# A layer of a hybrid decoder on one core: attention over the prompt's heads, their group norm and the output projection placed earlier in a schedule of 128 steps

## What is computed

```python
q_sb, k_sb, v_sb, q_fx, k_fx, v_fx, f = split(rms_norm(x) @ w_in)
# prompt, each head: 256 x 256 scores, stick breaking or softmax with a forget bias
o_sb = stick_breaking(q_sb, k_sb, v_sb); o_fx = forgetting(q_fx, k_fx, v_fx, cumsum(logf))
# samples: the same over cache + own token, 8 samples x 2048 past tokens x 16 heads
y = concat(rms_norm(o_sb) * g_sb, rms_norm(o_fx) * g_fx) @ w_out      # group norm, output pass
h = x + y
out = rms_norm(h + hierarchical_moe(rms_norm(h)))    # 32 experts, two for each token
# also returned: k and v of every head, prompt and sample, and the log forget values
```

## Time and profile before

| | us |
|---|---|
| median of 3 runs (1520.18 to 1528.28) | 1526.38 |
| the profiled execution, device time | 1525.93 |
| its span in the trace | 1524.2 |
| PE busy | 1339.2 (88%) |
| DVE busy | 676.4 (44%) |
| ACT busy | 243.5 (16%) |
| DMA, mean over the span | 370 GB/s |

### The profile page before, as it was taken

One profiled execution on the slowest core, in us unless ns is written; L12 is line 12 of the kernel. 1 busy time (PEld: TensorE's weight loads), 2 busy tenths in 40 slices (PEclk: granted clock), 3 DMA queues, 4 the chain that ended last, 5 costly groups with the idle time before them and its releaser, 6 DMA issues. The chain is left out here.

```text
span 1524.2 us, 27421 instructions
## 1 busy us (share of the span) xinstructions
PE 1339.2 (88%) x8718; PEld 891.7 (59%) x8718; DVE 676.4 (44%) x4802; ACT 243.5 (16%) x466; POOL 73.2 (5%) x119
## 2 busy tenths in 40 slices
PE   7999887889889889856999986889999999999992
PEld 5776554666556556523677753466567555665561
DVE  4657554676766757767655465312100100001004
ACT  2121111321321212112000011201101110111011
POOL 1000000000000000001000000101110010001000
PEclk8999999999999999977999997769999999999996
DMA  9789999999999999999899879589999999999984
GB/s 321 266 325 405 405 383 391 387 372 393 383 385 392 374 389 395 383 404 385 340 338 350 331 287 344 232 324 377 422 427 428 428 428 418 424 418 415 418 346 177
DMA packets 159080, 564.19 MB, mean 370 GB/s; under 512 B 17353, under 2 KB 59130, under 8 KB 145642
## 3 DMA queue, kind: packets, MB, share of 16 engines
q1 hardware_dynamic: 134304, 535.41, 89.6%
q10 hardware_dynamic: 21762, 22.58, 4.3%
q0 software_dynamic: 2896, 4.86, 1.0%
HBM read 551.97 MB, written 15.67 MB: 372 GB/s over the span
## 5 line engine op out<-in xcount | busy, mean ns | idle before, releaser
L132 DVE CUSTOM_DVE_ANT_0 ws<-ws,xgT 128x128 f32<-128x128 f32 x2048 | 443.3, 284 | 182.5 <-DMA ws<-in_cache_sb_k 108.1
L955 PE MATMUL bank<-xn,ws 128*128 128x264 f32 x1024 | 255.9, 406 | 4.3 <-DMA ws<-in_w_in 4.3
L955 PEld LDWEIGHTS bank<-xn,ws 128*128 128x128 f32 x1024 | 197.6, 198 | 90.9 <-issue 53.2
L1959 PE MATMUL bank<-ws,xgT 128*64 128x256 f32 x1024 | 231.1, 385 | 17.8 <-DMA ws<-in_w_expert_up 13.1
L1961 PE MATMUL bank<-ws,xgT 128*64 128x256 f32 x1024 | 231.2, 386 | 0.0
L911 PE MATMUL bank<-ws,PR 128*32 128x512 f32 x1024 | 152.4, 676 | 67.8 <-DMA ws<-in_cache_sb_v 43.6
L1959 PEld LDWEIGHTS bank<-ws,xgT 128*64 128x64 f32 x1024 | 140.0, 139 | 105.5 <-issue 21.7
L132 DVE DVE_READ_ACCUMULATOR2_ANT Z<- 128x1 f32 x2048 | 161.9, 79 | 0.0
L1961 PEld LDWEIGHTS bank<-ws,xgT 128*64 128x64 f32 x1024 | 140.3, 139 | 0.0
L2160 DVE COPY gu<-bank 128x256 f32<-128x256 f32 x32 | 13.6, 425 | 270.1 <-PE bank L1961 270.1
L1073 PE MATMUL bank<-qo,ws 128*128 128x256 f32 x512 | 118.6, 392 | 3.6 <-DVE qo L1565 3.6
(11 more groups left out here) (417 smaller groups left out, 1044.5 us busy)
## 6 DMA issues: line engine op xcount, KB each, us to landing
ws<-in_cache_sb_k SPq DMA_DIRECT2D x128, 512.0 KB, 8.6
ws<-in_cache_sb_v SPq DMA_DIRECT2D x128, 512.0 KB, 9.0
ws<-in_cache_fox_k SPq DMA_DIRECT2D x128, 512.0 KB, 8.8
ws<-in_cache_fox_v SPq DMA_DIRECT2D x128, 512.0 KB, 8.7
ws<-in_w_expert_down SPq DMA_DIRECT2D x32, 2048.0 KB, 17.0
ws<-in_w_expert_gate SPq DMA_DIRECT2D x32, 2048.0 KB, 16.0
ws<-in_w_expert_up SPq DMA_DIRECT2D x32, 2048.0 KB, 20.6
ws<-in_w_in SPq DMA_DIRECT2D x24, 2048.0 KB, 17.6
```

The costliest lines, as they stand in the source:

```text
L132: ins = dve.tensor_tensor_reduce(k, k, qb[:, m % 2, h * HD:(h + 1) * HD], 1.0, 0.0, ALU.mult, ALU.add, Z[:, m % 2, h, 2 * j + i:2 * j + i ...
L955: mm = pe.matmul(out[:, 0:T], w[:, c, m * P:(m + 1) * P], xn[:, c, :], start=(c == 0), stop=(c == KC - 1))
L1959: pe.matmul(bank[2 * k][0:SLOTS, 0:256], lhs, ws[:, wg, c * 256:(c + 1) * 256], start=(c == 0), stop=(c == KC - 1))
```

## The change

Three constants and the order of a head's pieces change.

- `UNIT0` goes from 24 to 20, so every prompt head starts four steps sooner; the last one ends in step 83 and not 87. `GSUM` goes from 89 to 85 and `OUT` from 92 to 88 with it.
- The output pass takes two of every three steps, 88, 89, 91, 92 and so on. `OUT_END`, `ROUTE` and `PLACE` stay at 111, 115 and 122.
- `ASKED` goes from 6 to 7: a query broadcast is in steps 7, 11, 15, ...
- A head's key is turned in piece 1 and its value in piece 2 (before: 0 and 1). DVE copies and ACT stores each a piece later as well, so the value's store stands in piece 3. The copies of the samples' own columns (`QK`, `VN`) move along.

```diff
-ASKED = 6
+ASKED = 7
...
-UNIT0 = 8 * (Q_TURNS + 1)
+UNIT0 = 8 * Q_TURNS + 4
...
-OUT_END = OUT + KC + KC // 4 - 1
+OUT_END = OUT + 3 * KC // 2 - 1
...
-    return d // 5 * 4 + d % 5 if 0 <= d < OUT_END - OUT and d % 5 < 4 else None
+    return d // 3 * 2 + d % 3 if 0 <= d < OUT_END - OUT and d % 3 < 2 else None
...
@@ PE, prompt_head
                     scores_read(pe, u - 1)
-                    wait_past(pe, S["row"], 2 * u)
                     z = bank[ZB]
...
+                elif piece == 1:
+                    wait_past(pe, S["row"], 2 * u)
                     rows(key)
-                elif piece == 1:
+                elif piece == 2:
                     pe.wait_ge(S["evac"], 4 * Q_TURNS + 4 * (u // 2) + u % 2 + 3)
                     pe.wait_ge(S["row"], 2 * u + 1)
                     rows(val)
-                elif piece == 2:
                     rest_read(pe, u - 1)
...
@@ ACT, prompt_head
-                elif piece == 1:
+                elif piece == 2:
                     act.wait_ge(S["row"], 2 * u + 1)
                     store(krow, fxk_p if g else sbk_p, fxk_s if g else sbk_s, h, "stk")
-                elif piece == 2:
...
+                elif piece == 3:
                     act.wait_ge(S["row"], 2 * u + 2)
                     store(vrow, fxv_p if g else sbv_p, fxv_s if g else sbv_s, h, "stv")
-                else:
                     act.wait_ge(S["o"], u + 1)
...
@@ DVE, prompt_head: in piece 1, behind that piece's arithmetic
+                    dve.wait_ge(S["tr"], 2 * u + 1)
+                    wait_past(dve, S["stk"], 32 * u)
+                    row_copy(krow)
...
@@ DVE, prompt_head: in piece 2, behind that piece's arithmetic
                     dve.wait_ge(S["tr"], 2 * u + 2)
                     wait_past(dve, S["stv"], 32 * u)
                     wait_past(dve, S["o"], u)
                     row_copy(vrow)
```

More of the change, by code:

```diff
@@ L1521, in prompt_head @@
                         dve.tensor_reduce(nmax[:, 1:2], zf[:, P:384], AX, ALU.max, negate=True).then_inc(S["zf"], 1)
[L1522 to L1528, removed]
                 elif piece == 1:
@@ L1539, in prompt_head @@
                         dve.tensor_scalar(pf[:, P:384], pf[:, P:384], rinv[:, 1:2], None, ALU.mult).then_inc(S["pn"], 1)
+                    dve.wait_ge(S["tr"], 2 * u + 1)
+                    wait_past(dve, S["stk"], 32 * u)
+                    row_copy(krow)
+                    if g:
+                        dve.tensor_tensor(QK[:, h, :], qo[:, H + h, SEQ:T], key_of(u)[:, SEQ:T], ALU.mult).then_inc(S["own_kv"], 1)
+                elif piece == 2:
+                    if g == 0:
+                        dve.wait_ge(S["C"], h + 1)
+                        own.step(dve.tensor_copy(pos_z[:, :], bank[CB][:, 0:384]))
+                        own.step(dve.scalar_tensor_tensor(out=att[:, :], in0=bank[ZB][:, 0:384], scalar=SCALE, in1=pos_z[:, :],
+                                                          op0=ALU.mult, op1=ALU.subtract))
+                        diag_op(att, neg_sb, ALU.add).then_inc(S["t"], 1)
                     dve.wait_ge(S["tr"], 2 * u + 2)
@@ L1543, in prompt_head @@
                     row_copy(vrow)
[L1544 to L1549, removed]
+                    if g:
+                        dve.tensor_copy(VN[:, h, :], vT[u % 2][:, SEQ:T]).then_inc(S["own_kv"], 1)
             def tt(out, x, y, op):
```

## The result

The changed kernel takes 1509.49 us in the median (11 runs, 1501.88 to 1516.24), the kernel before 1526.23 beside it (11 runs, 1519.84 to 1531.64). The ratio is 0.9895, with a 95% interval of 0.9867 to 0.9922: 12 to 20 us faster. 1508 was forecast. The profiled execution of the changed kernel took 1501.88 us and is the fastest of its eleven, 24.1 us shorter in span than the one before, so only a part of that difference is the change.

| | before | after | less |
|---|---|---|---|
| start to step 24 | 261.5 | 259.4 | 2.1 |
| step 24 to step 115 | 643.9 | 627.2 | 16.7 |
| step 115 to step 127 | 61.6 | 60.5 | 1.1 |
| step 127 to the end (experts) | 557.2 | 553.0 | 4.2 |

A forecast was written before the change was run, and what follows sets the result against it. Transfers were taken to bound steps 24 to 79 and PE the output pass, with DMA idle about 23 us there. 27.0 - 5.1 - 4 = 17.9; 1525.9 - 17.9 + 0.4 = 1508.4, so 1508 us; 8-in-10 range 1499 to 1520.

The forecast's parts named there:

- Limit of the heads' steps: Steps 24 to 79: transfers are the limit, and PE's idle 3.1 us a head covers new waits at no cost.
- When group norm starts: After the last head, DVE scores steps 84 to 87 from 681.7; group norm starts at 698, 27.0 us sooner.
- From group norm to the first product: The first output matmul stays 5.5 us behind group norm's start, at about 703.5.
- What now stands behind the first product: Work of steps 89 to 91, formerly ahead of the first output matmul, costs PE 5.1 us behind it.
- Whether DMA can follow: To step 115, transfers fit with 5 to 12 us spare; bursts cost 0 to about 11, taken as 4.
- rival 1: DMA takes the bound in the output pass: 11 us lost and not 4, so 1515, up to 1520; chance 0.22.
- Sum: Total gain over the kernel before: 27.0 - 5.1 - 4 = 17.9 us, giving 1508.
- The rival on POOL: POOL's preparation, busy 5.39 us, falls on group norm and holds it for all of that: 1513; chance 0.02.
- The cap: Without fewer bytes, the gain up to step 115 is capped at about 23 us, the output pass's idle DMA.

The follow-up runs named there:

- the five other kernels with this output pass: Changed kernel with later turning undone, `w_out` on SP, late key pages halved by columns, idle transposes, or broadcast in piece 2: 0.9925, 0.9924, 0.9901, 0.9889, 0.9887 of the kernel before.
- the columns: Changed kernel with key pages from step 92 on loaded only in the first 512 of 1024 columns, all partitions: 1511.64 us, 0.9901 of the kernel before.
- the kernel with four in five: Changed kernel with the output pass from step 88 in four of five steps, not two of three: 1521.64 us, 0.9983 of the kernel before.
- The best version here that leaves nothing out: Changed kernel with the second slice of `w_out` issued by ACT in step 87, not step 80: 1505.71 us, 0.9870 of the kernel before.
- the lighter products of the kernel before: Kernel before with one of eight channel chunks left out of every output product: 1513.79 us, 0.9937 of the kernel before.

## Why the prediction was right, step by step

- **Limit of the heads' steps.** Right. 390.8 us for 389.7, DMA share 1.03, SP waiting 0.9 us in all. The new waits were to cost nothing: undoing them, adding PE work and moving the broadcast back all changed nothing that the times can tell.
- **When group norm starts.** The mechanism was right, the term too large. 27.0 us sooner was forecast, 698; it was 700.70, and counted from step 24 it came 22.3 us sooner (463.53 to 441.26). The step that was off is the one that let DVE score steps 84 to 87 back to back from 681.7 on, with all pages there. DVE started even sooner, at 679.9, but waited 6.0 us for key pages in steps 86 and 87. The stores had landed by 697.0, when POOL starts, near the forecast 698. The prediction had bounded these steps by ACT, by DVE's pace and by the stores, and not by the bytes. Moving `w_out` to SP freed ACT and left the start where it was; with 2.1 MB less ahead of it as well it came 3.9 us sooner.
- **From group norm to the first product.** 5.5 us forecast, 5.53 measured.
- **What now stands behind the first product.** 5.1 us forecast. From the first output matmul to step 115 it was 174.86 us before and is 180.33 now, 5.5 more.
- **Whether DMA can follow.** 4 us were taken off for pages coming in bursts. It is nothing: PE is busy 159.57 of 159.70 us from step 91 on, in the five other kernels with this output pass it waits at most 0.6 us for pages there, and fewer bytes (the columns) make nothing faster. The lower bound of this term was the right one. Its upper bound was not added up rightly: 160 us at 386 GB/s and half of 23 us, less the 164.6 that PE wants, is 7 us and not 11, so rival 1 was priced 4 us too high. The first key pages behind group norm went out even later than forecast, at 716.22 for 712.9, and PE waited for none of the pages behind them. The spacing of two in three is what keeps it at nothing, as the kernel with four in five shows; the forecast had costed the spacing only by the slices of `w_out`.
- **Sum.** 22.3 - 5.5 - 0 = 16.8 at step 115, for 27.0 - 5.1 - 4 = 17.9. Two terms were too large, by 4.7 and by 4 us, with opposite signs. That the sum came so close, 1509.49 us for 1508, is luck in these two terms and not in the path, which was the forecast one. Behind step 115 nothing was given back (60.5 us for 61.6).
- **The rival on POOL.** POOL's preparation ran at 697.0 to 703.0, beside the last scores and the first two operations of group norm, and not beside its 16 products, which began at 705.59. The two took 0.75 and 3.40 us, for 0.77 and 3.40 before, and the products 6.49 both times. Rival 5, with 0.02 of the chances, was the author's estimate that POOL might hold group norm for all the 5.39 us for which it was busy in steps 88 to 91, which with the forecast gives 1513. No run shows such a hold. What they show is smaller: beside POOL two of the 16 score products of step 87 took 0.37 and 0.36 us and one 0.31, where the others took 0.28 or 0.29. In none of the kernels here did the 16 products of group norm meet POOL, so what they would take beside it is not shown.
- **The cap.** Idle DMA time as the cap of the gain was put at 23 us. The best version here that leaves nothing out was 23.4 us ahead at step 115, at the cap within what a profile tells. One kernel at the cap does not prove it.

What stays open: how far the heads' steps can be loaded before they become PE's; why half pages to half of the partitions made all transfers slower; why the lighter products of the kernel before show only 9.6 us in the times; and whether the later slice of `w_out` is a gain by the clock.

## What to carry to other kernels

Look for two neighbouring stretches with different limits, and move work of the one's busy engine into the other's idle time: the idle time of the resource that is short afterwards is a fair first cap of the gain. The earlier start and the spacing belong together, since in a dense block (four steps of five) a ring of four slots held the transfers back, to a DMA share of 0.87, and they had to be caught up when it ended. When an engine seems held by another ahead of such a move, ask first whether the bytes in flight allow the earlier time at all. A load that is not needed yet is worth moving: it brought group norm 3.9 us forward here. And before a single profile is read to a few us, compare it from the entry of the step where the edit begins, and look at the granted clock beside it: the change's own profile was the fastest of its eleven runs.

## What the hardware showed that was not expected

A key page of 512 KB to 128 partitions landed in a median of 9.6 us in the kernel with half pages, in the steps that still had whole ones. The half page, 256 KB to 64 partitions, took 13.9 us, and its stretch ran at a DMA share of 0.98 with 255 GB/s, against 0.80 with 290 GB/s where as many bytes were left out by columns on all partitions. Those 9.6 us are from other steps. Within steps 92 to 114, value and key pages of the changed kernel, then of the one with half pages (count, size, median us to landing):

```profile
ws<-in_cache_fox_v SPq DMA_DIRECT2D x42, 512.0 KB, 7.8
ws<-in_cache_fox_k SPq DMA_DIRECT2D x40, 512.0 KB, 9.4
```

```profile
ws<-in_cache_fox_v SPq DMA_DIRECT2D x46, 512.0 KB, 13.8
ws<-in_cache_fox_k SPq DMA_DIRECT2D x40, 256.0 KB, 15.4
```

The whole value pages, which the edit does not touch, slowed down from 7.8 to 13.8 us beside the half pages. With half of the columns the key pages took 7.0 us there and the value pages 6.9. Halving the partitions of a transfer saved nothing here, 15.4 us for 9.4, and slowed the others. No run here shows the cause.
